# Norm weights of q and k folded into rotation tables and a copy; transposed probabilities copied by VectorE

## The reference, cut to what matters

```python
q = partial_rope(rms_norm(q.reshape(B, S, 8, 2, 64), q_norm_g), cos, sin)
k = partial_rope(rms_norm(k.reshape(B, S, 8, 2, 64), k_norm_g), cos, sin)

def partial_rope(t, cos, sin):          # rotates the first 16 of the 64 channels
    rot, rest = t[..., :16], t[..., 16:]
    x1, x2 = rot[..., :8], rot[..., 8:]
    rot = concatenate([x1 * cos - x2 * sin, x2 * cos + x1 * sin], axis=-1)
    return concatenate([rot, rest], axis=-1)

s = einsum('bqhcd,bkhcd->bhcqk', q, k) * 64 ** -0.5
p = softmax(where(causal, s, -inf), axis=-1)
a = p[:, :, 0] - lam * p[:, :, 1]
o = einsum('bhqk,bkhe->bqhe', a, v)     # then rms_norm over the 128 channels
```

## Time and profile before

| | |
|---|---|
| runs | 1286.41, 1286.7, 1288.59 us (median 1286.7) |
| the profiled execution | 1286.41 us, its span 1284.6 us |
| TensorE matmul busy | 1080.6 us (84%) |
| VectorE busy | 404.4 us (31%) |
| ScalarE busy | 219.0 us (17%) |
| DMA moved | 475.81 MB, mean 370 GB/s |
| the chain that ended last | TensorE 49%, DMA 41%, SyncE's queue 5%, ScalarE 3%, VectorE 1% |

### The profile page before, as it was taken

The page is one execution under the profiler, slowest core; times in us unless marked ns, Lnnn a source line. Parts: engine busy times, 40 slices in busy tenths (PEclk is TensorE's granted clock), DMA queues, the critical chain, the costliest instruction groups (busy, mean ns, idle before and its releaser), DMA issues.

```text
span 1284.6 us, 23431 instructions
## 1 busy us (share of the span) xinstructions
PE 1080.6 (84%) x9958; PEld 528.3 (41%) x9958; DVE 404.4 (31%) x1129; ACT 219.0 (17%) x461; POOL 51.7 (4%) x91
## 2 busy tenths in 40 slices
PE   8999999899998566669998657968669696999975
PEld 5864458788433122224443212423224242444431
DVE  1388997631232111112222111212112121232221
ACT  1111124640121000002211001201002110122110
POOL 2000000355000000000000000000000000000000
PEclk9999999999999887889999888989889898999998
DMA  9998672256879999999999999999999999599997
GB/s 328 349 371 327 239 285 92 106 181 228 325 323 427 428 427 428 427 427 429 426 429 427 427 428 427 426 425 429 428 427 429 425 429 427 241 429 428 428 426 312
DMA packets 66084, 475.81 MB, mean 370 GB/s; under 512 B 6329, under 2 KB 19966, under 8 KB 39390
## 3 DMA queue, kind: packets, MB, share of 16 engines
q1 hardware_dynamic: 62100, 471.36, 89.2%
q0 software_dynamic: 816, 1.84, 0.5%
q10 hardware_dynamic: 3098, 1.56, 0.5%
HBM read 473.03 MB, written 1.05 MB: 369 GB/s over the span
## 4 chain that ended last, share of the span: by engine, by line
PE 49%; DMA 41%; SPq 5%; ACT 3%; DVE 1%; another core or an unknown queue 1%; issue 1%; ACTq 0%; DVEq 0%
DMA weights<-in_w_down 27%; PE bank L1556 14%; DMA weights<-in_w_up 13%; PE bank L1288 7%; PE bank L1584 7%; PE bank L1281 6%; SPq L462 4%; PE bank L1273 2%; PE bank L1426 2%; PE bank L1498 2%; PE bank L1224 2%; PE bank L1485 1%; PE bank L1194 1%; DMA weights<-in_w_ada 1%; PE bank L1505 1%
## 5 line engine op out<-in xcount | busy, mean ns | idle before, releaser
L1556 PE MATMUL bank<-weights,buf_d 128*32 128x512 f32 x3008 | 394.6, 671 | 141.6 <-DMA weights<-in_w_up 141.6
L1556 PEld LDWEIGHTS bank<-weights,buf_d 128*32 128x32 f32 x3008 | 96.9, 117 | 405.0 <-DMA weights<-in_w_up 211.5
L1584 PE MATMUL bank<-weights,buf_d 128*32 128x256 f32 x3008 | 177.6, 382 | 42.7 <-DMA weights<-in_w_down 39.9
L1165 DVE TENSOR_SCALAR u_conv<-bank 128x256 f32<-128x256 f32 x47 | 20.0, 425 | 467.5 <-PE bank L1556 467.5
L774 ACT ACTIVATE u_conv<-u_conv 128x256 f32<-128x256 f32 x47 | 19.6, 416 | 708.5 <-DVE u_conv L1165 708.5
L1584 PEld LDWEIGHTS bank<-weights,buf_d 128*32 128x32 f32 x3008 | 90.7, 110 | 115.5 <-DMA weights<-in_w_down 51.6
L864 DVE SCALAR_TENSOR_TENSOR weights<-u_conv,weights 128x256 f32<-128x256 f32 x240 | 97.8, 481 | 0.5
L1281 PE MATMUL bank<-weights,buf_d 128*128 128x512 f32 x192 | 82.9, 594 | 0.0
L1177 DVE TENSOR_TENSOR buf_d<-bank,u_conv 128x256 f32<-128x256 f32 x47 | 20.0, 425 | 180.1 <-PE bank L1584 180.1
L774 ACT ACT_TABLE_LOAD x47 | 60.3, 1283 | 1.4 <-issue 0.5
L1288 PE MATMUL bank<-buf_d,weights 128*128 128x256 f32 x256 | 58.6, 383 | 0.0
(11 more groups left out here) (274 smaller groups left out, 799.4 us busy)
## 6 DMA issues: line engine op xcount, KB each, us to landing
weights<-in_w_up SPq DMA_DIRECT2D x128, 2048.0 KB, 35.5
weights<-in_w_down SPq DMA_DIRECT2D x64, 2048.0 KB, 39.2
weights<-in_w_in SPq DMA_DIRECT2D x10, 2048.0 KB, 15.5
weights<-in_w_ada SPq DMA_DIRECT2D x8, 2048.0 KB, 19.3
weights<-in_w_ada SPq DMA_DIRECT2D x8, 1024.0 KB, 11.3
weights<-in_w_in SPq DMA_DIRECT2D x8, 512.0 KB, 10.1
weights<-in_w_in SPq DMA_DIRECT2D x4, 1024.0 KB, 13.1
weights<-in_w_conv_out SPq DMA_DIRECT2D x2, 2048.0 KB, 11.3
```

What stands on the lines that cost most here:

```text
L1556: ins = t.matmul(UP[SLOTS * g:SLOTS * g + SLOTS, :], xgT[:, r, SLOTS * j:SLOTS * j + SLOTS], up_group(w[:, r, :], g), start=False, stop=(j ...
L1584: ins = t.matmul(DOWN[rows, 0:T], actT[:, r, at:at + SLOTS], w[:, g, r, T * q:T * q + T], start=False, stop=(h == 1 and g == 1 and r == 1))
```

## The change

- The four loads of `q_norm_g` and `k_norm_g` (each twice, for the two parts) are added to ScalarE's first loads, four places ahead of the end of that list. They land in rows 26 and 27 of `col_rows`, and TensorE waits for 15 loads in place of 11.
- Column 28 of `cols` becomes the product of the two weights, with 1 in the places of the rotated channels: one product and two memsets on VectorE, each followed by a wait for its end.
- Six VectorE operations build `turns`, tables of cos and sin multiplied by the rotated channels' weights, for q and for k, ahead of the first q tile.
- For each of the 8 tiles the product with the norm weights (L931) goes; the rotation is two products of 128x128 with the tables and two additions of 128x64.
- ScalarE's four copies to `kT` become activations with the column 28 as scale.
- `keep_aT` goes from ScalarE to VectorE. There it stands where VectorE waited for the transposition, behind L979 and L980 and ahead of L985; for head 7 it stands behind the loop, ahead of the last `keep_o`.

```diff
@@ -131,7 +131,8 @@
         qk_g = early[:, 3456:3584].rearrange("p (i e) -> p i e", i=2)
-        rot = early[:, 3584:3840].rearrange("p (i g j) -> p i g j", i=4, g=8)
+        rot = early[:, 3584:3840].rearrange("p (i g j) -> p i g j", i=2, g=8)
+        turns = early[:, 3968:4096].rearrange("p (w i t h j) -> p w i t h j", w=2, i=2, t=TT, h=2)
         rope = early[:, 3840:3968].rearrange("p (i t j) -> p i t j", i=8, t=TT)
@@ -606,6 +607,9 @@
             load(col_rows[24:25, :], subln_g, in_cols)
+            for i, w in enumerate((q_norm_g, k_norm_g)):
+                for half in range(2):
+                    load(col_rows[26 + i:27 + i, HD * half:HD * half + HD], w, in_cols)
             load(col_rows[40:56, :], b_gate[0].rearrange("(k p) -> k p", p=P), in_cols)
@@ -672,13 +676,9 @@
                 dst = (qT if i < 4 else kT)[:, 2 * (i % 4):2 * (i % 4) + 2, :]
-                s.copy(dst, bank(QKT_USE + i)[:, :].rearrange("p (h t) -> p h t", h=2)).then_inc(
-                    bank_free[(QKT_USE + i) % 4], 1)
-
-            def keep_aT(h):
-                use = aT_use(h)
-                full(act_e, use)
-                s.copy(aT[:], bank(use)[:, 0:384]).then_inc(bank_free[use % 4], 1)
+                src = bank(QKT_USE + i)[:, :].rearrange("p (h t) -> p h t", h=2)
+                ins = s.copy(dst, src) if i < 4 else s.activation(dst, src, ACT.Copy, scale=cols[:, 28:29])
+                ins.then_inc(bank_free[(QKT_USE + i) % 4], 1)
 
@@ -697,8 +697,6 @@
                                      bias=smax[:, par, at:at + 1], accum_out=ssum[:, par, at:at + 1]).then_inc(exp_done, 1)
-                if h:
-                    keep_aT(h - 1)
                 use = gate_use(h)
@@ -718,7 +716,6 @@
                                      bias=cols[:, 16 + k:17 + k]).then_inc(sw_sig, 1)
-            keep_aT(HEADS - 1)
             attended(HEADS - 1)
@@ -827,6 +824,9 @@
                     step(v.tensor_scalar(cols[:, 25:26], cols[:, 24:25], SUBLN, None, ALU.mult))
+                    step(v.tensor_tensor(cols[:, 28:29], cols[:, 26:27], cols[:, 27:28], ALU.mult))
+                    for half in range(2):
+                        step(v.memset(cols[HD * half:HD * half + ROT, 28:29], 1.0))
 
@@ -914,6 +914,14 @@
             dve.wait_ge(rope_ready, 1)
+            for which in range(2):
+                gain_rot = qk_g[:, which, 0:ROT].rearrange("p (h j) -> p h j", h=2)
+                places = [P, TT, 2, HALF]
+                step(v.tensor_tensor(turns[:, which, 0, :, :, :], rope[:, 6, :, :].unsqueeze(2).to_broadcast(places),
+                                     gain_rot.unsqueeze(1).to_broadcast(places), ALU.mult))
+                step(v.tensor_tensor(turns[:, which, 1, :, :, :], rope[:, 7, :, :].unsqueeze(2).to_broadcast(places),
+                                     gain_rot.unsqueeze(1).to_broadcast(places), ALU.mult))
+                step(v.tensor_scalar(turns[:, which, 1, :, 1, :], turns[:, which, 1, :, 1, :], -1.0, None, ALU.mult))
             between = ([(1, 8, 13)], [(1, 13, 18)], [(1, 18, 23)], [(1, 23, 28)], [(1, 28, TAPS), (2, 0, 2)],
@@ -928,16 +936,15 @@
                 dve.wait_ge(bank_free[use % 4], use // 4 + 1)
-                step(v.tensor_tensor(dst, dst, qk_g[:, which, :].unsqueeze(1).to_broadcast([P, 8, HD]), ALU.mult))
-                cos = rope[:, 6, tt, :].unsqueeze(1).to_broadcast([P, 8, HALF])
-                sin = rope[:, 7, tt, :].unsqueeze(1).to_broadcast([P, 8, HALF])
-                x1, x2 = dst[:, :, 0:HALF], dst[:, :, HALF:ROT]
-                v.tensor_tensor(rot[:, 0, :, :], x1, cos, ALU.mult)
-                v.tensor_tensor(rot[:, 1, :, :], x2, sin, ALU.mult)
-                v.tensor_tensor(rot[:, 2, :, :], x2, cos, ALU.mult)
-                step(v.tensor_tensor(rot[:, 3, :, :], x1, sin, ALU.mult))
-                v.tensor_tensor(x1, rot[:, 0, :, :], rot[:, 1, :, :], ALU.subtract)
-                v.tensor_tensor(x2, rot[:, 2, :, :], rot[:, 3, :, :], ALU.add).then_inc(qk_ready, 1)
+                x = dst[:, :, 0:ROT]
+                for j in range(2):
+                    turn = turns[:, which, j, tt, :, :].rearrange("p h j -> p (h j)").unsqueeze(1).to_broadcast([P, 8, ROT])
+                    ins = v.tensor_tensor(rot[:, j, :, :], x, turn, ALU.mult)
+                step(ins)
+                for j in range(2):
+                    ins = v.tensor_tensor(dst[:, :, HALF * j:HALF * j + HALF], rot[:, 0, :, HALF * j:HALF * j + HALF],
+                                          rot[:, 1, :, HALF - HALF * j:ROT - HALF * j], ALU.add)
+                ins.then_inc(qk_ready, 1)
                 for stretch in between[i]:
@@ -955,6 +962,11 @@
             conv(3, 11, 19)
+
+            def keep_aT(h):
+                use = aT_use(h)
+                full(dve, use)
+                v.tensor_copy(aT[:], bank(use)[:, 0:384]).then_inc(bank_free[use % 4], 1)
 
@@ -980,7 +992,7 @@
                 if h:
-                    full(dve, aT_use(h - 1))
+                    keep_aT(h - 1)
                 for blk_q, (a, b) in enumerate(((0, P), (P, 3 * P))):
@@ -1005,6 +1017,7 @@
                                     ALU.mult).then_inc(ln_ready, 1)
+            keep_aT(HEADS - 1)
             keep_o(HEADS - 1)
@@ -1233,7 +1246,7 @@
                          maskb[:, P:2 * P].unsqueeze(1).to_broadcast([P, 4, P]), start=True, stop=True, skip_group_check=True)
-            pe.wait_ge(in_cols, 16 * 11)
+            pe.wait_ge(in_cols, 16 * 15)
             rest = TAPS * KD - P
```

## The result

The changed kernel takes 1291.16 us (median of 8 runs, 1290.47 to 1292.27), the kernel before in the same runs 1286.87 (1286.41 to 1288.59). The ratio is 1.0031, with a 95% interval of 1.0022 to 1.0040: slower by 4.0 us, between 2.8 and 5.1.

A forecast was written before the change was run, and what follows sets the result against it. TensorE was taken to bound the head loop and DMA the experts, with dense-part losses arriving whole. Terms 0.40 + 0.61 + 2.10 + 0.57 = 3.68 us, so 1286.7 + 3.7 = 1290.4 us; range 1287.0 to 1292.6.

The forecast's parts named there:

- What bounds the kernel: Head loop bound by TensorE, experts by DMA; a microsecond won or lost in the dense part arrives at the end whole.
- The covered case: Rival: the experts' stream of loads covers the dense part's loss, the 3.7 us vanish, 1286.7 us; chance 0.10.
- The copy to `aT`: Head loop: VectorE's later, slower copy costs 0.61 in pass 2, 2.10 in passes 4 to 6, 0.57 us behind the loop.
- kT copies: Ahead of the first scores: four ScalarE copies with a scale cost 0.10 us more each, +0.40 us.
- Norm product and rotation: Ahead of 180 us: VectorE comes some 6 us earlier to the modulation rows but waits there for TensorE; value 0.
- that case: Rival: the convolution gets ahead, waits of passes 4 to 6 shrink, at best 1282.8 us; chance 0.08.
- The loads: At the start: four more parameter loads delay TensorE's first transposes by 1.34 us, which fits in its slack; value 0.
- The late-parameter case: Rival: the added loads land 8.6 us after issue, +3.3 us more, 1293.7 us; chance 0.05.

The follow-up runs named there:

- run 5: Kernel before with ScalarE's copy to `aT` put ahead of its wait for the maxima and the exponentials in passes 2, 4, 5 and 6: 1284.17 us, ratio 0.9978.
- run 8: Changed kernel with the stretch `conv(3, 11, 19)` moved ahead of the turned modulation rows, into VectorE's idle 6.5 us: 1290.89 us, ratio 1.0027 to the kernel before.
- run 3: Changed kernel with VectorE's copy directly behind the wait for the exponentials, ahead of the inverse and the scaling: 1288.68 us, ratio 1.0017 to the kernel before.
- run 6: Changed kernel with VectorE's copy ahead of its wait for the exponentials in passes 2, 4, 5 and 6: 1283.9 us, ratio 0.9977 to the kernel before.
- run 7: Changed kernel with the copy back on ScalarE, ahead of the exponentials in passes 2, 4, 5 and 6: 1283.93 us, ratio 0.9980 to the kernel before.
- run 4: Kernel before with only the four small parameter loads added and waited for, their values unused: 1286.77 us, ratio 1.0000.
- run 1: Kernel before with only the copy to `aT` moved to VectorE: 1290.53 us, ratio 1.0036.
- run 9: Changed kernel with eight small matmuls, their result overwritten, ahead of TensorE's wait of pass 4: 1291.27 us, ratio 1.0033 to the kernel before.
- run 2: Changed kernel with only the copy to `aT` given back to ScalarE in its old place: 1287.97 us, ratio 1.0007 to the kernel before.
- run 10: Changed kernel with early `aT` copy on ScalarE, `conv(3, 11, 19)` ahead, three of eight q and k copies on VectorE: 1284.02 us, ratio 0.9977 to the kernel before.
- run 11: Kernel before with ScalarE's `aT` copy early in passes 2, 4, 5 and 6, and the last copy ahead of the squares of head 6: 1284.02 us, ratio 0.9974.
- run 12: Changed kernel: early ScalarE `aT` copy, last ahead of head 6's squares; convolution ahead; q and k copies shared, scale on q: 1283.59 us, ratio 0.9975 to kernel before.

## Why the prediction was right, point by point

**What bounds the kernel.** Right. The staircase ends at +4.86 us and the span at +4.9; in the other direction run 5 starts the experts 3.0 us earlier and ends 2.8 earlier. Over all fourteen profiles the experts start between 360.14 and 369.24 us, and from there to the end of the span it is always 921.0 to 922.4. The covered case, with 0.10, is out: what the dense part wins or loses arrives at the end.

**The copy to `aT`.** Right in mechanism and size. The wait rows, as predicted and as measured without a fall of the clock (run 8, which has the changed kernel's copy): pass 2 0.61 and 0.46; pass 4 2.11 and 2.10; pass 5 1.74 and 1.74; pass 6 1.64 and 1.65; behind the loop 1.48 and 1.46. Together 7.6 and 7.4. Passes 1, 3 and 7 add nothing, as said: the changed kernel's rows stand behind by 0.86, 1.55 and 4.30 us there (202.62, 222.31 and 266.73), within 0.1 us of what they stand behind just ahead. The 0.56 us for the copy, taken from two other shapes' slope, was 0.557. The Trainium skill (ScalarE: Activation LUTs, Rules for kernel authors) prefers VectorE for simple elementwise work, as up to about three times faster in bf16. Had that held for this copy, it would have been shorter than ScalarE's 0.49 us; the row decides for 0.557, in float32 out of PSUM. In run 3 the copy's own duration was unchanged and the loss about halved, so the order counted for more than the engine; runs 6 and 7 show it outright.

**kT copies.** +0.40 was forecast, and 1.60 - 1.25 = 0.35 measured at the scores. The scaled copy has a mean of 0.728 us and is a little costlier than L729's 0.689.

**Norm product and rotation.** Right: L942 has 0.288 (0.29 forecast), VectorE idles 6.5 us (a little over the 5 to 6 forecast), and it is worth nothing. Run 8 shows that it is worth nothing even when VectorE spends that time on later work; the prediction had given that case 0.08.

**The loads.** The value 0 was right (run 4). L1251 starts at 12.94 us, within the 13.06 worked out; its counterparts in the other nine profiles with these loads start between 12.78 and 13.33, so the worked-out bound was a little too tight. The late-parameter case, with 0.05, did not come.

**What the sum missed.** Taken off the staircase of the profiled execution: 0.35 at the scores, 0.62 in pass 2, 0.77 in pass 4, 0.70 of pass 5, 0.72 in pass 6, 0.56 behind the loop: 3.72, against 3.68 forecast. To the 4.86 there are 1.14 missing. Of these 0.50 stand at the start, and by run 4 that is scatter of the one execution. The other 0.64 are in pass 5's step of 1.34: behind its 2.10 us wait TensorE ran at the lower clock, and from its first `attend` matmul to ScalarE's squares of the result it was 1.57 us (233.86 to 235.43), where pass 5 at the full clock has 0.94 (246.19 to 247.13). Run 8, with the same waits up to there and no fall, confirms the size: it is 0.14 us ahead of the changed kernel at the first scores, in pass 2 and in pass 4, and 0.78 ahead from pass 5 on. The prediction had counted the idle time itself and nothing for what follows it. That term was missing, not mis-sized. It would explain that the medians lie 4.3 us apart where 3.7 was said, if the clock fell in the timed executions too; no profile shows that, and the difference is within the interval of the ratio (2.8 to 5.1 us).

## What to carry to other kernels

Ask of a moved operation not only how long it takes on the new engine but what that engine does just ahead of it: here two tiny operations and the handover of a semaphore made up 0.62 of the 0.69 us that a pass lost, the longer copy only 0.07, and the same copy ahead of a wait, on either engine, won 2.5 us and more. An instruction that needs nothing from a wait should stand ahead of it wherever its input is there; the order in the program is the queue. And before crediting an engine with saved time, find its next wait: 6.5 us of VectorE were saved here and turned into idle time at the next thing that TensorE delivers.

## What the runs showed of the hardware

In three profiles TensorE's granted clock fell from 2.4 GHz to 1.2 inside the head loop, for some 3.4 us: in the changed kernel and in run 1 behind the 2.1 us wait of pass 4, and in run 9, where that wait had been cut to 0.70, behind the 1.67 us wait of pass 6. In run 9 the eight score matmuls behind that wait took 1.50 us; in the changed kernel, at the full clock, the same eight took 0.93. Run 8 has the same waits as the changed kernel within 0.03 us in four of five and kept its clock, so the wait alone does not decide. In none of the profiles whose waits in the loop are at most 1.65 us (before and runs 2 to 7, 10 to 12) did the clock fall ahead of 300 us; in five of them (runs 2, 4, 6, 10 and 12) it fell between 358 and 364 us. What else decides is not settled. What a fall costs depends on what follows it: 0.64 us behind pass 4, where the next wait for the copy shrank from 1.74 us (run 8) to 0.77, and 1.64 us behind pass 6 in run 9, where no such wait followed.

An operation that waits for another engine starts a little behind its end: in pass 4 TensorE follows VectorE's copy by 0.15 us (233.71 to 233.86).
